# A two-block transformer on one core: expert loads asked for earlier, padding products moved ahead of TensorE's branch, two tables later

## What is computed

```python
def first_block(x, ...):
    for i in range(DEPTH):                      # DEPTH = 2
        m = even_mixer(x, ...) if i % 2 == 0 else odd_mixer(x, ...)   # attention, projections in and out
        x = layer_norm(DN_ALPHA * x + m, ln1_g[i], ln1_b[i])
        f = hier_moe(x, ...)                    # 32 experts, each token goes to 2 of them
        x = layer_norm(DN_ALPHA * x + f, ln2_g[i], ln2_b[i])
    return x

def second_block(x, ...):
    u = rms_norm_2(x, norm1_gain)
    proj = u @ w_in                             # 1024 x 3072
    ...                                         # recurrence, retention
    h = x + mixed @ w_out
    u = rms_norm_2(h, norm2_gain)
    up = causal_depthwise_conv(u @ ffn_up_w, ffn_conv_w, ffn_conv_b)
    return rms_norm_2(h + (gelu(a_branch) * v_branch) @ ffn_down_w, final_norm_gain)
```

## Time and profile before

| | |
|---|---|
| median of 3 runs | 1590.69 us (1589.97 to 1591.29) |
| the profiled execution's own time | 1588.95 us |
| its span | 1587.2 us |
| TensorE busy | 1515.0 us, 95% of the span |
| VectorE, ScalarE, GpSimd busy | 560.4, 459.6, 151.2 us |
| moved by DMA | 502.51 MB, mean 317 GB/s |
| granted TensorE clock, mean | 0.984 |

### The profile page before, as it was taken

The page is one execution under the profiler, slowest core; times in us unless marked ns, Lnnn a source line. Parts: engine busy times, 40 slices in busy tenths (PEclk is TensorE's granted clock), DMA queues, the critical chain, the costliest instruction groups (busy, mean ns, idle before and its releaser), DMA issues.

```text
span 1587.2 us, 19141 instructions
## 1 busy us (share of the span) xinstructions
PE 1515.0 (95%) x7664; PEld 888.6 (56%) x7664; DVE 560.4 (35%) x1130; ACT 459.6 (29%) x792; POOL 151.2 (10%) x124
## 2 busy tenths in 40 slices
PE   8989999999999988999999999999998899899997
PEld 6655454444445434975544444544434597588886
DVE  5754211121111113035512111111111468489974
ACT  4460111111111102444111111111110461387654
POOL 0211000000000002842100000000000340001200
PEclk9999999999999999999999999999999999999999
DMA  7624999999999999540799999999999654555410
GB/s 287 246 99 171 415 429 427 427 428 428 427 427 429 428 428 362 200 172 41 287 415 428 428 427 428 427 427 429 429 427 385 260 213 161 183 186 200 171 54 27
DMA packets 69673, 502.51 MB, mean 317 GB/s; under 512 B 4064, under 2 KB 5344, under 8 KB 43616
## 3 DMA queue, kind: packets, MB, share of 16 engines
q1 hardware_dynamic: 68736, 495.17, 75.9%
q0 software_dynamic: 864, 6.29, 1.0%
HBM read 500.40 MB, written 1.05 MB: 316 GB/s over the span
## 4 chain that ended last, share of the span: by engine, by line
PE 82%; DMA 10%; DVE 3%; issue 2%; ACT 2%; SPq 0%; DVEq 0%; ACTq 0%
PE bank L897 25%; PE bank L927 12%; PE bank L763 9%; DMA ring<-in_w_up 6%; PE bank L850 6%; PE bank L1158 6%; PE bank L728 5%; PE bank L1171 4%; PE bank L1160 3%; PE bank L864 3%; DMA ring<-in_w_gate 3%; PE bank L797 2%; PE bank L835 1%; PE bank L810 1%; PE bank L824 1%
## 5 line engine op out<-in xcount | busy, mean ns | idle before, releaser
L897 PE MATMUL bank<-ring,arena 128*64 128x512 f32 x1536 | 345.7, 606 | 21.0 <-issue 11.3
L897 PEld LDWEIGHTS bank<-ring,arena 128*64 128x64 f32 x1536 | 115.7, 139 | 245.7 <-issue 245.7
L927 PE MATMUL bank<-ring,arena 128*64 128x512 f32 x768 | 170.1, 595 | 2.4 <-ACT arena L1292 2.4
L1723 DVE TENSOR_TENSOR arena<-arena,bank 128x512 f32<-128x512 f32 x32 | 22.0, 687 | 393.9 <-PE bank L897 393.9
L1158 PE MATMUL bank<-x_split,w_high 128*128 128x512 f32 x384 | 134.7, 395 | 2.7 <-DVE x_split L1554 2.7
L850 PEld LDWEIGHTS bank<-SEL,x_by_row 128*128 128x128 f32 x1024 | 116.7, 192 | 25.8 <-issue 24.3
L850 PE MATMUL bank<-SEL,x_by_row 128*128 128x128 f32 x1024 | 122.8, 279 | 0.0
L1737 DVE SCALAR_TENSOR_TENSOR y_low<-bank,ST,y_high 128x512 fp32r<-128x512 f32 x64 | 48.0, 751 | 202.4 <-ACT y_high L1296 202.4
L1296 ACT ACTIVATE y_high<-bank,ST 128x512 fp32r<-128x512 f32 x64 | 44.0, 687 | 245.6 <-PE bank L927 245.6
L897 PE MATMUL bank<-arena 128*64 128x512 f32 x384 | 111.8, 592 | 0.0
L927 PEld LDWEIGHTS bank<-ring,arena 128*64 128x64 f32 x768 | 54.8, 137 | 100.9 <-issue 100.9
(11 more groups left out here) (305 smaller groups left out, 2229.2 us busy)
## 6 DMA issues: line engine op xcount, KB each, us to landing
ring<-in_w_gate SPq DMA_DIRECT2D x48, 2048.0 KB, 19.3
ring<-in_w_up SPq DMA_DIRECT2D x48, 2048.0 KB, 20.0
ring<-in_w_down SPq DMA_DIRECT2D x44, 2048.0 KB, 18.2
arena<-in_w_gate SPq DMA_DIRECT2D x12, 2048.0 KB, 19.7
arena<-in_w_up SPq DMA_DIRECT2D x12, 2048.0 KB, 20.1
arena<-in_w_down SPq DMA_DIRECT2D x12, 2048.0 KB, 20.2
ring<-in_ffn_up SPq DMA_DIRECT2D x12, 2048.0 KB, 8.9
ring<-in_w_in SPq DMA_DIRECT2D x9, 2048.0 KB, 12.9
```

Source lines behind the costliest of these rows:

```text
L897: last = nc.tensor.matmul(bank[4 + m][64 * e:64 * e + 64, :], XG[:, c, 64 * e:64 * e + 64], w[e][:, c, :], start=(c == 0), stop=(c == C - 1))
L927: last = nc.tensor.matmul(bank[6 + half][64 * e:64 * e + 64, :], HT[:, j, 64 * e:64 * e + 64], w[e][:, j, 512 * half:512 * half + 512], st ...
```

## The change

Four edits. In the first turn of `load_experts` the loads of places 6, 7, 8 are issued ahead of those of places 4, 5, and they wait for something earlier: in layer 0 for the transposes of the attention's output (`tr_done`), in layer 1 for the last product of attention (`a_pv`). The useless products at the head of `normed_and_first_chunk` go to the end of the layer's experts, ahead of TensorE's branch, 5 in layer 0 and 9 in layer 1 as before. The bias table is issued behind the fourth load of `w_qkv`, the two tables of the second block behind the third load of `w_in`.

```diff
-            def load_experts(l, arena_free):
-                for n in range(6 * AHEAD):
+            def load_experts(l, *arena_free):
+                first = [n for n in range(POOL) if n not in (4, 5, POOL - 1)] + [4, 5, POOL - 1]
+                for n in first + list(range(POOL, 6 * AHEAD)):
                     k, e, place = n % 6, n // 6 * 2 + n % 2, n % POOL
...
                     elif place < POOL - 1:
-                        sp.wait_ge(pj_done, arena_free)
+                        sp.wait_ge(*arena_free)
                     else:
                         sp.wait_ge(logits_done, l + 1)
...
-            load_experts(0, 2 * G_EO + 1)
+            load_experts(0, tr_done, sum(TR["ao"]))
             for i in I_QKV + I_OO:
                 load(i)
-                if i == I_QKV[0]:
+                if i == I_QKV[3]:
                     sp.dma_start(G[:, :, :], na_bias).then_inc(bias_loaded, 16)
-            load_experts(1, 2 * G_OO + 1)
+            load_experts(1, a_pv, B_HEADS + C_HEADS)
             for i in I_IN2 + I_OUT2 + I_UP + I_DN:
                 load(i)
-                if i == I_IN2[1]:
+                if i == I_IN2[2]:
                     sp.dma_start(KT2[:, :], table2).then_inc(table2_loaded, 16)
                     sp.dma_start(GATE[:, :, :], gates).then_inc(table2_loaded, 16)
...
-            def normed_and_first_chunk(name, source, ready, n0, s, before, after):
-
-                keep_clock(7, before)
+            def normed_and_first_chunk(name, source, ready, n0, s, after):
+
                 transposes_by_token(name, source, ready, n0, [0])
                 keep_clock(7, after)
...
                 scatter_by_half(n)
+                keep_clock(7, 9 if l else 5)
                 with pe.If(more > 0):
...
-            normed_and_first_chunk("ln1", X, x_ready, 2, S_QKV, 5, 2)
+            normed_and_first_chunk("ln1", X, x_ready, 2, S_QKV, 2)
...
-            normed_and_first_chunk("n1", XN, xn_ready, 0, S_IN2, 9, 4)
+            normed_and_first_chunk("n1", XN, xn_ready, 0, S_IN2, 4)
```

## The result

The changed kernel takes 1576.78 us (median, 1575.65 to 1577.47, 4 runs) against 1590.33 us of the kernel before in the same comparison. The ratio is 0.9919, with a 95% interval of 0.9906 to 0.9932: 12.9 us less, by the interval 10.8 to 14.9. A second comparison gave 0.9928 (0.9912 to 0.9943). Forecast were 12.1 us less. The profiled execution took 1575.65 us, its span is 1573.8 us.

A forecast was written before the change was run, and what follows sets the result against it. TensorE and transfers together were taken to bound the experts, TensorE's sequencer the borders; 1588.95 - 6.0 - 6.1 = 1576.8 us for the profiled execution, 1578.6 us for the median, range 1574.5 to 1584.0.

The forecast's parts named there:

- What bounds the borders: Behind each layer's experts TensorE's sequencer is the limit: a branch of 6.862 or 6.141 us, then useless products ahead of T0.
- Price of the products: Ahead of the branch the useless matmuls run at 0.43 us each: about 4.3 us in border 0, 7.7 in border 1.
- The branch runs under them: At both borders the branch starts within 0.2 us of its present start, under the products, until 619.0 and 1242.3 us.
- Rival 3: At both borders the branch waits until the products are done: slower, 1594.3 us together; chance 0.07.
- lasts as long: The branch behind the experts keeps its length with products ahead of it: 6.86 us in border 0, 6.14 in border 1.
- What is late next: Border 0: T0 waits for the branch, L763 gains 6.0 us. Border 1: L763 waits for VectorE, gains 6.1 us.
- Early places and tables at nothing: Earlier expert loads gain nothing, since the stream restarts at the request at 191.59 us; later bias and tables change nothing.
- The clock in border 0: Whether TensorE's clock falls during 2.2 us without work between the products' end and T0; forecast steady at 0.44.
- Rival 1: The clock falls ahead of T0 in border 0, T0 to L763 takes 5.2 us: 2.5 us lost, 1581.1 us; chance 0.30.
- The sum: Whole kernel: gains of 6.0 and 6.1 us at the borders, profiled execution 1576.8 us, median 1578.6 us.
- One sign of being wrong: The prediction would be wrong if the experts of a layer took less time than before.

The follow-up runs named there:

- the dose in the other direction: Changed kernel with the loads of places 6, 7, 8 issued behind places 4 and 5, later than in the kernel before: 0.9943 against the kernel before.
- fifteen upstream: Changed kernel with 15 more useless products ahead of the last expert pair's up products, where TensorE waits for a load: 1593.88 us, one run.

## Why the prediction was right

**What bounds the borders.** Right. The products left the path, and TensorE's 6 us behind the branch are now covered.

**Price of the products.** Right: 4.46 and 7.89 us (the last matmul's modelled end included) for 4.3 and 7.7.

**The branch runs under them.** Right in what mattered here, that it starts at once: 612.4 and 1228.5, with L876. The run-ahead of 20 matmuls that the step used was measured as 18. Rival 3 is refuted by the run with 20 products too. The step's second half, that it "lasts as long" as before, was 0.8 us too long in border 0 (6.05 for 6.86); hence 6.9 us gained there instead of 6.0. The 6.86 wasn't steady: with none to nine products ahead of it the branch took 5.97 to 6.94 us, and 6.27 in border 0 with the tables alone, where TensorE's program is that of before. That it lasted about as long at all was in part luck: the step gave no reason, and the length hangs on how much code stands ahead of the branch. Seven products more in border 0 halved it, eleven more in border 1 took it away.

**What is late next.** Right in border 1: L763 waits for VectorE's low parts, 6.2 us gained for 6.1. In border 0 T0 was forecast behind the branch and waits for the norm, which ends close beside it.

**Early places and tables at nothing.** Right, by 0.9999 and 0.9995; and for the reason given for the places: the hole at 192 us opened, and in the trace the dose in the other direction cost 2.5 to 2.7 us a layer. That the tables moved nothing is measured; why was not looked into.

**The clock in border 0.** Rival 1 had 0.30 and did not come: TensorE idled 1.25 us ahead of T0 by its row, not 2.2, and the clock stayed at 1.00. In the six other traces with the products ahead of the branch in this number and place, T0 to L763 takes 2.69 to 2.77 us as well, so it was steady there too.

**The sum.** 12.1 us forecast, 12.9 measured, which is less apart than the interval is wide. In the pair of traces the borders gave 13.1; of the 1.0 more, 0.8 is the branch's length in border 0. One sign of being wrong that the prediction named did appear: layer 1's experts took 1.7 us less than before. That is the chance of a clock fall and no effect of the change, as the 11 of 20 layers above show.

## What to carry to other kernels

Put useless products that keep TensorE's clock up ahead of a branch that holds the sequencer and not behind it: here they ran ahead of it at the full clock in time that was lost anyway, and behind it at half clock on the path. Look first whether they are worth their place: here most of the gain was that they left the path. When a branch takes microseconds, compare its end with the packets on the queue for instructions: here it was waiting for code, and more code ahead of it hid the fetch. Before counting on an earlier load, look whether the stream behind it has a dip at the next request that waits for computing: if it has, the stream starts again there and the earlier load gives nothing. And when a norm on the path has two operands in SBUF, see when the GpSimd instruction beside it ends. Before a single row is used as the price of a step, look at it in a second trace: the branch's length in border 0 was 6.27, 6.86 and 6.94 us in three traces of the same TensorE program.

## What the runs showed of the hardware that I had not expected

The compare-and-branch that skips the overflow rounds takes from 0.33 to 6.94 us depending on how much code stands in front of it, not on what it does: 5.97 to 6.94 us with none to nine products, 3.03 and 6.34 with twelve, 0.35 and 0.34 with twenty, 0.35 and 0.33 with fifteen upstream. Whenever it is held, it ends 1.36 to 1.55 us after a 16 KB packet has landed on the queue for instructions.

VectorE's multiply-add over 128x1024 with two tensors in SBUF takes 2.8 us beside GpSimd's subtraction and 1.28 alone, and when it is held it ends 1.08 us behind GpSimd's instruction, however much of it overlaps. L1613, with one operand in a bank, takes 1.41 us for two of 128x512 beside GpSimd, and 1.40 without it (before, at 627.58). The Trainium skill, "VectorE: DVE Perf Modes", Two Vector instructions with no wait between them, says that an instruction with two SBUF tensors reads one through an interface that it shares with GpSimd; the trace agrees with that, with these two pairs of numbers. Of what the norm does in the time that it is held, the trace shows no more than its end.

Without products TensorE idled 5.5 and 8.2 us ahead of T0, and the lower level of the clock (1.2 GHz) cost only 1.3 and 1.0 us up to L763: the full clock was granted again 3.7 and 5.0 us behind T0.
